# A float32 encoder trunk on one core: seven block products instead of eight for the first two up blocks of each MLP chunk

## The chip, the cores and the metric

The kernel runs on one core of one Trainium2 chip. The metric is the device time of one execution in microseconds. The engines are PE (TensorE: matmuls, with the loads of the stationary operand shown as PEld), DVE (VectorE), ACT (ScalarE), POOL (GpSimd) and SP (SyncE, which issues the loads of the weights). Each works through its own queue in program order and waits on semaphores.

## The reference

256 tokens of width 2048 pass two layers. Each layer has a mixer and then an MLP, both with an RMS norm in front and a residual add behind:

```
h = rmsnorm(x, norm_mix_w);  x = x + mixer(h)       # layer 0: retention and RG-LRU, layer 1: window attention
h = rmsnorm(x, norm_mlp_w)
u = relu(h @ w_up)           # 2048 -> 8192
x = x + (u * u) @ w_down     # 8192 -> 2048
```

The mixer ends with an output projection of 2048 columns, whose result is added to `x`. Everything is float32.

## The kernel before

**Tiling.** A block is 512 output columns over a contraction of 2048 (16 pieces `kt` of 128 rows), for both tiles of 128 tokens (`tt` 0 and 1). The program is a list of 89 blocks: 12 of the mixer's input, 4 residual blocks (`res`, numbered r0 to r3 here), 32 of an MLP, 5 of attention's input, 4 residual blocks, 32 of an MLP. An MLP runs in 4 chunks of 4 up blocks and 4 down blocks. The MLP's middle chunks are loops, the rest is written out.

**Precision.** Each float32 operand is split into a high part, which ACT rounds, and a rest, which DVE subtracts; a product is then three matmuls: high by high, high by low, low by high (lines 1399 to 1401). A block is read as 8 halves of two `kt`; a half is 12 matmuls of 128x128 by 128x512. For each half ACT makes `w_hi` (line 733, called a *hi* here) and DVE makes `w_lo` (line 976, a *lo*) from the raw weights in `raw`. Both have a ring of 4 halves, so ACT may make the *hi* of step k+4 when PE has done step k.

**Ticks.** ACT and DVE run a loop over the same steps: at tick k each first does what stands in `post` for the block before (evacuation, transposes, splitting), then the *hi* or *lo* of step k+4. What stands ahead of a *hi* or *lo* in its queue delays it.

**Pairs.** In the first three chunks of each MLP the four down blocks go as two pairs. Of the 2x2 blocks (two token tiles by the first four `kt` in two parts, by two column blocks) a pair makes seven products P1 to P7 of 6 matmuls each (`product`, lines 1425 to 1427) in place of two halves of two blocks (48 matmuls). The order of a pair's 20 steps is `PAIR_STEPS`: products, the halves 2 to 7 of the left (L) and the right (R) block, and an empty step. The products take token sums (`s_hi`, `s_lo`, made by `add_tokens`, `tokens`, `tokens_rest`) and weight sums, which DVE makes in `raw` (`add_weights`, lines 987 to 994). Four intermediate results are added to `x` by DVE (`add_part`, line 1003). R accumulates in `acc`, L in `bank`.

**Up blocks.** ACT takes an up block out of PSUM with the norm's scale and Relu (line 783), squares it in `stage` (line 788), DVE transposes it by 16 instructions of 32x256 into `turn` (line 1219), ACT and DVE split it into `b_hi` and `b_lo` (lines 741 and 1029), the stationary operands of the down blocks.

**Residual blocks.** DVE adds a residual block to `x` (line 1238), ACT takes its square sums (line 753), DVE transposes it by 16 instructions, ACT and DVE make `a_hi` (lines 743, 744) and `a_lo` (line 1033) with the norm's weights. The norm's factor is applied when an up block leaves. At the start of an MLP the first two up blocks are woven: PE does 6 halves of the first and 2 of the second before the two halves that need r3, and it waits for r0 to r2 before the first:

```
WOVEN_ORDER = ([(0, k) for k in range(6)] + [(1, 0), (1, 1), (0, 6), (0, 7)]
               + [(1, k) for k in range(2, 8)])
```

**Loads.** SP loads the weights by 1 MB (a unit: two halves) into four places of `raw`; each load waits until the *lo* of the last step that read its place is done.

Of the kernel before, what the change touches and what calls it, by code (L numbers as in the profile page):

```python
# [23 lines left out]
ACT = mybir.ActivationFunctionType  # L24
# [45 lines left out]
def mlp_blocks(last_kind):  # L70
    blocks = []
    for c in range(CHUNKS):
# [19 lines left out]
BY_QUADRANT = {"up", "res"} | DIRECT  # L92
# [9 lines left out]
QUADRANTS_PAIR = {6: 4, 7: 4, 8: 4, 9: 4}  # L102
# [7 lines left out]

PAIR_CHUNKS = CHUNKS - 1
PAIRS0 = {m + PERIOD * c + COLS + 2 * n for m in (MLP0, MLP1) for c in range(PAIR_CHUNKS) for n in range(2)}
PAIRS1 = {b + 1 for b in PAIRS0}
FIRST_PAIRS = {m + PERIOD * c + COLS for m in (MLP0, MLP1) for c in range(PAIR_CHUNKS)}
PAIR_STEPS = [("P", 1), ("L", 2), ("P", 5), ("L", 3), ("P", 2), ("P", 6), ("P", 4), ("L", 4), ("P", 7),
              ("L", 5), ("P", 3), ("R", 2), ("R", 3), ("R", 4), ("R", 5), ("R", 6), ("R", 7), (None, 0),
              ("L", 6), ("L", 7)]
PAIR_SPLIT = 17
STEP_OF = {what: k for k, what in enumerate(PAIR_STEPS)}
PAIR_UNITS = [("L", 0), ("R", 0), ("L", 1), ("L", 2), ("R", 1), ("R", 2), ("R", 3), ("L", 3)]  # L120
PAIR_FREE = [STEP_OF["P", 4] + 1, STEP_OF["P", 3] + 1, STEP_OF["L", 3] + 1, STEP_OF["L", 5] + 1,
             STEP_OF["R", 3] + 1, STEP_OF["R", 5] + 1, STEP_OF["R", 7] + 1, STEP_OF["L", 7] + 1]
# [3 lines left out]
LAST_TURNED_AT = STEP_OF["R", 6]  # L126
# [3 lines left out]
NSTEP = [PAIR_SPLIT if b in PAIRS0 else len(PAIR_STEPS) - PAIR_SPLIT if b in PAIRS1 else HALVES  # L130
         for b in range(NBLK)]
STEP0 = [sum(NSTEP[:b]) for b in range(NBLK + 1)]

# [14 lines left out]
def pair_step(b, k):  # L148

    if b in PAIRS0:  # L150
        return PAIR_STEPS[k]
    if b in PAIRS1:
        return PAIR_STEPS[PAIR_SPLIT + k]
    return None


def weight_at(b, k):

    what = pair_step(b, k)
    if what is None:  # L160
        return k // 2, k % 2, b + 1
    side, h = what
    first = b if b in PAIRS0 else b - 1
    if side == "P":
        q, e = PIECE_OF[h]
        return q, e, first + 1
    n = PAIR_UNITS.index((side, h // 2))
    return n % UNITS, h % 2, first + 1 + n // UNITS
WOVEN_ORDER = ([(0, k) for k in range(6)] + [(1, 0), (1, 1), (0, 6), (0, 7)]
# [70 lines left out]
SUMS_AT = {1: 0, 2: 1, 4: 2, 5: 3}  # L240
N_EVAC_ACT = total(BY_ACT, TT)
# [16 lines left out]
class Slot:  # L258
# [69 lines left out]
def build(nc, t):  # L328
    ctx = ExitStack()
    with ctx:  # L330
# [67 lines left out]
        place["at"] = 0  # L398
        kk_t = take(KV, SEQ)
# [12 lines left out]
        s_sum = take(4, 2, P)  # L412
# [89 lines left out]
        tokens_lo = sem("tokens_lo")  # L502

# [42 lines left out]
        def _(sp):  # L546
# [31 lines left out]
            def load(slot, view):  # L578

                b0 = slot.b  # L580
                for q in range(UNITS):
                    if b0 in PAIRS0:
                        side, g = PAIR_UNITS[q]
                        d = 0 if side == "L" else 1
                    elif b0 in PAIRS1:
                        side, g = PAIR_UNITS[UNITS + q]
# [5 lines left out]
                    if b0 in PAIRS1:  # L592
                        free = PAIR_FREE[q] - PAIR_SPLIT
                    elif b0 - 1 in PAIRS1:
                        free = PAIR_FREE[UNITS + q] - len(PAIR_STEPS)
                    else:
                        free = 2 * q + 2 - HALVES
# [116 lines left out]
        def _(act):  # L714
            def cut_hi(slot, n):
# [14 lines left out]
                if STEP0[slot.b] + n >= RING:  # L730
# [3 lines left out]
                                     ACT.Copy).then_inc(hi_ready, 2 if what == ("R", HALVES - 1) else 1)  # L734
# [25 lines left out]
            def leave(slot, kind, j):  # L760

                b = slot.b - 1
                act.wait_ge(half_used, slot.halves(late(b)))
# [5 lines left out]
                for tt in range(TT):  # L769
                    src = acc[:, b % 2, tt, :]  # L770
# [11 lines left out]
                    else:  # L782
                        ins = nc.scalar.activation(stage[:, tt, :], src, ACT.Relu if kind == "up" else ACT.Copy, scale=s)
                    ins.then_inc(evac_act, 1)
                if kind == "up":
# [63 lines left out]

            def post(slot, k):  # L850
                b = slot.b - 1
                if b < 0:
                    return
                kind, j = BLOCKS[b]
                if b - 1 + COLS in FIRST_PAIRS and k == 6:
                    tokens(slot)
                if k == late(b) and kind in BY_ACT:
                    leave(slot, kind, j)
                if k == 1 + late(b) and kind in ("res", "fin"):
                    act.wait_ge(evac_dve, slot.count(N_EVAC_DVE, 0))  # L860
                    square_sums(next_norm(b), j)
                if kind in SPLIT and k == out_at(kind, b):
                    hi, _, kt, scale = target(b)
                    for m in range(2):
                        turned_parts(hi, kt + 2 * m, None if scale is None else scale + 2 * m,
                                     slot.count(N_MOVED, -1, INIT_HALVES + m + 1), m, kind in BY_QUADRANT)
                if k == 4 and kind == "res" and j == COLS - 1:
# [89 lines left out]
        def _(dve):  # L957
# [8 lines left out]
            def cut_lo(slot, n):  # L966
# [5 lines left out]
                if what == (None, 0):  # L972
# [5 lines left out]
                                        ALU.subtract).then_inc(lo_ready, 2 if what == ("R", HALVES - 1) else 1)  # L978
# [18 lines left out]
            def add_part(slot, k):  # L997

                left, right = (slice((BLOCKS[slot.b + d][1]) * NB, (BLOCKS[slot.b + d][1] + 1) * NB) for d in (0, 1))
                for p, tt, cols, src in ((1, 0, left, 1), (5, 1, right, 0), (6, 0, right, 1), (7, 1, left, 1)):  # L1000
                    if k == STEP_OF["P", p]:
                        dve.wait_ge(half_used, slot.halves(k + 1))
                        nc.vector.tensor_tensor(x[:, tt, cols], x[:, tt, cols], accumulator(slot.b, src),
                                                ALU.add).then_inc(part_added, 1)

            def add_tokens(slot):

                a = turn[:, :, :].rearrange("p m (k t s) -> p m t k s", k=2, t=TT)
                (a11, a21), (a12, a22) = ([a[:, m, tt] for tt in range(TT)] for m in range(2))
# [6 lines left out]
                nc.vector.tensor_tensor(s4, a12, s2, ALU.subtract).then_inc(tokens_added, 1)  # L1016

# [176 lines left out]
            def turn_quadrants(slot, k, kind, j):  # L1194


                at = {tick + late(slot.b - 1): n for tick, n in quadrants_at(kind, slot.b - 1).items()}
# [11 lines left out]
                src = x[:, :, j * NB:(j + 1) * NB] if kind == "res" else stage  # L1209
# [13 lines left out]

            def plain_target(kind, j):
# [3 lines left out]
            def post(slot, k):  # L1228
                b = slot.b - 1
                if b < 0:  # L1230
                    return
                kind, j = BLOCKS[b]
                if k == late(b) and kind in ("res", "down", "fin"):
                    dve.wait_ge(half_used, slot.halves(late(b)))
                    for tt in range(TT):
                        c = BLOCKS[b + (b in PAIRS0) - (b in PAIRS1)][1]
                        xs = x[:, tt, c * NB:(c + 1) * NB]
                        nc.vector.tensor_tensor(xs, xs, accumulator(b, tt), ALU.add).then_inc(evac_dve, 1)
                if k == 1 + late(b):
# [18 lines left out]
                if kind in BY_QUADRANT:  # L1258
                    turn_quadrants(slot, k, kind, j)
# [475 lines left out]
```

## Time and profile before

| | before |
|---|---|
| time, median of 3 runs | 1993.46 us (1993.35 to 1993.85) |
| the profiled execution | 1995.09 us, its span 1993.3 us |
| PE busy | 1984.1 us (100%), 9089 instructions |
| PE weight loads | 1638.8 us (82%) |
| DVE busy | 1581.1 us (79%), 2190 instructions |
| ACT busy | 1066.0 us (53%), 1402 instructions |
| POOL busy | 45.1 us (2%) |
| HBM | 379.34 MB read, 191 GB/s over the span |

Busy times of different engines overlap. Matmuls are pipelined: a record lasts about 0.39 us, while the next one starts 0.227 us after it. In a timeline a row gives the start, the length (of several merged instructions, from the first's start to the last's end), the engine, the line, the operation and the tiles, and in brackets the idle time before it. The time between the starts of two instructions that follow each other without a wait is called their pace here; it is less than the duration.

### The profile page before, as it was taken

How to read it: one execution, taken by the hardware profiler on the slowest of the kernel's cores; microseconds unless marked ns; L12 is line 12 of the kernel's file. 1: busy time of each engine (PE TensorE's matmuls, PEld its weight loads, DVE VectorE, ACT ScalarE, POOL GpSimd, SP SyncE). 2: the span in 40 equal slices, each digit the busy share in tenths (PEclk: the TensorE clock that was granted, in tenths of full speed). 3: DMA queues.
4: the chain of work that ended last, by engine and by line, in shares of the span. 5: the costliest groups of instructions: out<-in, count | busy, mean ns of one | idle time of the engine just before them, and what ended most of it. 6: DMA issues, size and time to landing. Idle time of an engine off the chain costs nothing.

```text
span 1993.3 us, 25055 instructions
## 1 busy us (share of the span) xinstructions
PE 1984.1 (100%) x9089; PEld 1638.8 (82%) x9089; DVE 1581.1 (79%) x2190; ACT 1066.0 (53%) x1402; POOL 45.1 (2%) x55
## 2 busy tenths in 40 slices
PE   9999999999999999999999999999999999999998
PEld 7888888888888888888888878888888888888887
DVE  6777678989769868976889887989858876985875
ACT  6665665555445545544545566555445544544554
POOL 1110110000000000000000000000000000000000
PEclk9999999999999999999999999999999999999999
DMA  8556545655665475556655545564575555466563
GB/s 306 177 182 205 181 165 203 202 172 192 217 199 170 168 249 182 184 206 190 211 190 186 174 154 165 182 197 152 197 247 191 188 206 189 148 218 226 187 205 112
DMA packets 191758, 382.50 MB, mean 192 GB/s; under 512 B 6328, under 2 KB 7616, under 8 KB 191552
## 3 DMA queue, kind: packets, MB, share of 16 engines
q1 hardware_dynamic: 190288, 377.51, 56.5%
q0 software_dynamic: 1216, 3.88, 0.6%
q8 instruction: 48, 0.79, 0.2%
q14 instruction: 30, 0.25, 0.0%
q10 hardware_dynamic: 176, 0.07, 0.0%
HBM read 379.34 MB, written 2.10 MB: 191 GB/s over the span
## 4 chain that ended last, share of the span: by engine, by line
PE 98%; DVE 1%; issue 0%; ACT 0%; DMA 0%; ACTq 0%
PE acc L1399 26%; PE acc L1400 26%; PE acc L1401 26%; PE bank L1399 3%; PE bank L1400 3%; PE bank L1401 3%; PE acc L1426 1%; PE acc L1425 1%; PE acc L1427 1%; DVE area L1219 1%; PE bank L1427 1%; PE bank L1425 1%; PE bank L1426 1%; PE bank L1515 0%; PE bank L1592 0%; PE bank L1616 0%
## 5 line engine op out<-in xcount | busy, mean ns | idle before, releaser
L976 DVE TENSOR_TENSOR w_lo<-raw,w_hi 128x1024 fp32r<-128x1024 f32 x744 | 899.8, 1223 | 354.4 <-ACT w_hi L733 350.1
L733 ACT ACTIVATE w_hi<-raw 128x1024 fp32r<-128x1024 f32 x744 | 777.2, 1059 | 716.7 <-PE acc L1401 562.4
L1399 PE MATMUL acc<-w_hi,a_hi 128*128 128x512 f32 x1552 | 607.1, 391 | 0.0
L1401 PE MATMUL acc<-w_hi,a_lo 128*128 128x512 f32 x1552 | 604.1, 389 | 0.0
L1400 PE MATMUL acc<-w_lo,a_hi 128*128 128x512 f32 x1552 | 604.0, 389 | 0.0
L1399 PEld LDWEIGHTS acc<-w_hi,a_hi 128*128 128x128 f32 x1552 | 291.5, 188 | 61.2 <-issue 0.9
L1401 PEld LDWEIGHTS acc<-w_hi,a_lo 128*128 128x128 f32 x1552 | 291.4, 188 | 60.8
L1400 PEld LDWEIGHTS acc<-w_lo,a_hi 128*128 128x128 f32 x1552 | 291.4, 188 | 59.9
L1399 PE MATMUL acc<-w_hi,b_hi 128*128 128x512 f32 x784 | 305.7, 390 | 0.0
L1400 PE MATMUL acc<-w_lo,b_hi 128*128 128x512 f32 x784 | 305.3, 389 | 0.0
L1401 PE MATMUL acc<-w_hi,b_lo 128*128 128x512 f32 x784 | 305.0, 389 | 0.0
L1219 DVE STREAM_TRANSPOSE turn<-stage 32x256 f32<-32x256 f32 x512 | 223.0, 436 | 7.8
L1399 PEld LDWEIGHTS acc<-w_hi,b_hi 128*128 128x128 f32 x784 | 147.2, 188 | 32.2 <-issue 0.9
L1401 PEld LDWEIGHTS acc<-w_hi,b_lo 128*128 128x128 f32 x784 | 147.2, 188 | 30.7
L1400 PEld LDWEIGHTS acc<-w_lo,b_hi 128*128 128x128 f32 x784 | 147.2, 188 | 30.2
L1400 PE MATMUL bank<-w_lo,b_hi 128*128 128x512 f32 x288 | 112.5, 391 | 0.0
L1399 PE MATMUL bank<-w_hi,b_hi 128*128 128x512 f32 x288 | 112.5, 391 | 0.0
L1401 PE MATMUL bank<-w_hi,b_lo 128*128 128x512 f32 x288 | 112.3, 390 | 0.0
L741 ACT ACTIVATE b_hi<-turn 128x512 fp32r<-128x512 f32 x64 | 37.0, 625 | 112.5 <-DVE turn L1219 112.5
L1219 DVE STREAM_TRANSPOSE turn<-x 32x256 f32<-32x256 f32 x192 | 83.6, 435 | 2.9
L1399 PEld LDWEIGHTS bank<-w_hi,b_hi 128*128 128x128 f32 x288 | 54.0, 188 | 12.1
L1401 PEld LDWEIGHTS bank<-w_hi,b_lo 128*128 128x128 f32 x288 | 54.1, 188 | 11.7
(240 smaller groups left out, 1296.8 us busy)
## 6 DMA issues: line engine op xcount, KB each, us to landing
raw<-in_mlp_w_up SPq DMA_DIRECT2D x128, 1024.0 KB, 5.4
raw<-in_mlp_w_down SPq DMA_DIRECT2D x128, 1024.0 KB, 5.1
raw<-in_hyb_w_in SPq DMA_DIRECT2D x44, 1024.0 KB, 5.3
raw<-in_attn_w_qkv SPq DMA_DIRECT2D x20, 1024.0 KB, 5.1
raw<-in_hyb_w_out SPq DMA_DIRECT2D x16, 1024.0 KB, 5.2
raw<-in_attn_w_out SPq DMA_DIRECT2D x16, 1024.0 KB, 5.1
raw<-in_hyb_w_in SPq DMA_DIRECT2D x5, 512.0 KB, 9.6
out_y<-x SPq DMA_DIRECT2D x4, 512.0 KB, 3.0
```

The lines of the kernel that those rows point to most:

```text
L733: nc.scalar.activation(w_hi[:, ring(b, h)], raw[:, q, 2 * e:2 * e + 2, :], ACT.Copy).then_inc(hi_ready, 2 if what == ("R", HALVES - 1) else 1)
L741: nc.scalar.activation(hi[:, kt:kt + 2, :], src, ACT.Copy).then_inc(turned_hi, 1)
L976: nc.vector.tensor_tensor(w_lo[:, ring(b, h)], raw[:, q, 2 * e:2 * e + 2, :], w_hi[:, ring(b, h)].bitcast(F32), ALU.subtract).then_inc(lo_ ...
L1219: ins = nc.vector.transpose(dst[f * QUAD:(f + 1) * QUAD, :, :, a, :], src[a * QUAD:(a + 1) * QUAD, :, :, f, :])
L1399: nc.tensor.matmul(a, xh, wh, start=first, stop=False, skip_group_check=joins)
L1400: nc.tensor.matmul(a, xh, wl, start=False, stop=False, skip_group_check=joins)
L1401: ins = nc.tensor.matmul(a, xl, wh, start=False, stop=last, skip_group_check=joins)
L1425: nc.tensor.matmul(a, xh, wh, start=first, stop=False, skip_group_check=True)
L1426: nc.tensor.matmul(a, xh, wl, start=False, stop=False, skip_group_check=True)
L1427: ins = nc.tensor.matmul(a, xl, wh, start=False, stop=False, skip_group_check=True)
```

## The change

The first two up blocks of every chunk, in all four chunks of both MLPs, become a pair too (`UP0`, `UP1`), with an order of their own: the L block is finished first. The first pair of an MLP follows the residual blocks directly and takes r0 as the operand of its products; PE waits for r2 at L4 and for r3 at L6. The token sums of r0 are made once per MLP by DVE (`add_up_tokens`, from `a_hi + a_lo`), kept in `s_up`, and split into `s_hi` and `s_lo` again for each chunk, in the second down pair of the chunk before. The four intermediate results of an up pair are copied by DVE into `part_l` and `part_r`, the rest is added there (`sum_pair`), and ACT applies Relu in place.

The transposes change, too. For every up block but `UP0`, and for r1 to r3 of both layers, ACT writes 16 pieces of 32x256 to other partitions (`squares`, `move_res`: the square is made on the way, or a copy), in `shifted`; DVE then transposes by 4 instructions of 128x256 (`turn_shifted`). The ticks of these pieces stand in tables. The square sums and the norm of r3 go from ticks 1 to 5 to ticks 11 to 14.

The core of the diff:

```diff
-BY_QUADRANT = {"up", "res"} | DIRECT
+BY_QUADRANT = {"res"} | DIRECT
+BY_VECTOR = BY_QUADRANT | {"up"}
...
+QUADRANTS_UP = {3: 4, 4: 4, 6: 4, 7: 4}
+SQUARES_UP0 = {2: 2}
+SQUARES_UP1 = {1: 2, 2: 4, 3: 2, 4: 4, 5: 4}
+SQUARES_AT = {0: 4, 1: 6, 2: 6}
+SQUARES_PAIR = {3: 2, 4: 2, 5: 2, 6: 2, 7: 2, 8: 2, 9: 2, 10: 2}
+RES_AT = {2: 2, 3: 4, 4: 1, 5: 1, 6: 2, 7: 5, 8: 1}
+RES_MOVED_AT = {1: 4, 2: 4, 3: 4, 4: 4}
+LAST_SUMS_AT = 11
...
+UP0 = {m + PERIOD * c for m in (MLP0, MLP1) for c in range(CHUNKS)}
+UP1 = {b + 1 for b in UP0}
+DOWN0 = {m + PERIOD * c + COLS + 2 * n for m in (MLP0, MLP1) for c in range(PAIR_CHUNKS) for n in range(2)}
+DOWN1 = {b + 1 for b in DOWN0}
+PAIRS0, PAIRS1 = UP0 | DOWN0, UP1 | DOWN1
+MIXED = [("P", 1), ("L", 2), ("P", 5), ("L", 3), ("P", 2), ("P", 6), ("P", 4), ("L", 4), ("P", 7),
+         ("L", 5), ("P", 3), ("R", 2), ("R", 3)]
+DOWN_STEPS = MIXED + [("R", 4), ("R", 5), ("R", 6), ("R", 7), (None, 0), ("L", 6), ("L", 7)]
+UP_STEPS = MIXED + [("L", 6), ("L", 7), (None, 0), ("R", 4), ("R", 5), ("R", 6), ("R", 7)]
...
+UP_UNITS = [("L", 0), ("R", 0), ("L", 1), ("L", 2), ("R", 1), ("L", 3), ("R", 2), ("R", 3)]
...
+def squares_at(b):
+
+    if before_mlp(b):
+        return RES_AT
+    if moved_by_act(b):
+        return {k + late(b): n for k, n in RES_MOVED_AT.items()}
+    if b in UP0 | UP1:
+        return SQUARES_UP0 if b in UP0 else SQUARES_UP1
+    return SQUARES_PAIR if b + 1 in FIRST_PAIRS else {k + late(b): n for k, n in SQUARES_AT.items()}
+
...
+            def squares(slot, k):
+
+                b = slot.b - 1
+                at = squares_at(b)
+                if k not in at:
+                    return
+                if k == min(at):
+                    act.wait_ge(evac_act, slot.count(N_EVAC_ACT, 0))
+                if b in UP0:
                     for tt in range(TT):
-                        act.wait_ge(evac_act, slot.count(N_EVAC_ACT, -1, tt + 1))
-                        nc.scalar.activation(stage[:, tt, :], stage[:, tt, :], ACT.Square).then_inc(squared, 1)
+                        ins = nc.scalar.activation(part_l[:, tt, :], part_l[:, tt, :], ACT.Square)
+                    ins.then_inc(squared, 1)
+                    return
+                src = up_stage(b).rearrange("p t (k f c) -> p t k f c", k=COLS, f=QUADRANTS)
+                done = sum(n for tick, n in at.items() if tick < k)
+                for n in range(done, done + at[k]):
+                    a, f = divmod(n, QUADRANTS)
+                    ins = nc.scalar.activation(shifted[f * QUAD:(f + 1) * QUAD, a], src[a * QUAD:(a + 1) * QUAD, :, :, f, :],
+                                               ACT.Square)
+                if k == max(at):
+                    ins.then_inc(squared, 1)
+
+            def move_res(slot, k, j):
+
+                b = slot.b - 1
+                at = squares_at(b)
+                if k not in at:
+                    return
+                if k == min(at):
+                    act.wait_ge(evac_dve, slot.count(N_EVAC_DVE, 0))
+                src = x[:, :, j * NB:(j + 1) * NB].rearrange("p t (k f c) -> p t k f c", k=COLS, f=QUADRANTS)
+                done = sum(n for tick, n in at.items() if tick < k)
+                for n in range(done, done + at[k]):
+                    a, f = divmod(n, QUADRANTS)
+                    ins = nc.scalar.activation(shifted[f * QUAD:(f + 1) * QUAD, a], src[a * QUAD:(a + 1) * QUAD, :, :, f, :],
+                                               ACT.Copy)
+                if k == max(at):
+                    ins.then_inc(res_moved, 1)
...
+            def up_tokens(slot):
+
+                act.wait_ge(up_added, 1 if slot.b < MLP1 - 1 else 2)
+                if slot.b in DOWN0:
+                    act.wait_ge(half_used, slot.halves(STEP_OF["P", 3] + 1))
+                nc.scalar.activation(s_hi[:, :, :, :], s_up[:, :, :, :], ACT.Copy).then_inc(up_hi, 1)
...
+                b = slot.b
+                right = side_block(b, "R")
+                for p, side, tt, src in ((1, 0, 0, 1), (5, 1, 1, 0), (6, 1, 0, 1), (7, 0, 1, 1)):
                     if k == STEP_OF["P", p]:
                         dve.wait_ge(half_used, slot.halves(k + 1))
-                        nc.vector.tensor_tensor(x[:, tt, cols], x[:, tt, cols], accumulator(slot.b, src),
-                                                ALU.add).then_inc(part_added, 1)
+                        if b in UP0:
+                            ins = nc.vector.tensor_copy((part_l, part_r)[side][:, tt, :], accumulator(right, src))
+                        else:
+                            j = BLOCKS[b + side][1]
+                            xs = x[:, tt, j * NB:(j + 1) * NB]
+                            ins = nc.vector.tensor_tensor(xs, xs, accumulator(right, src), ALU.add)
+                        ins.then_inc(part_added, 1)
+
+            def sum_pair(slot, b):
+
+                part = up_stage(b)
+                dve.wait_ge(part_added, slot.pairs(4, 4, pair_of(b)[0]))
+                for tt in range(TT):
+                    nc.vector.tensor_tensor(part[:, tt, :], part[:, tt, :], accumulator(b, tt),
+                                            ALU.add).then_inc(pair_summed, 1)
+
...
+            def add_up_tokens(slot):
+
+                whole = part_l.rearrange("p t n -> p (t n)").rearrange("p (k s) -> p k s", k=4)
+                dve.wait_ge(turned_out, slot.count(N_TURNED, -1, INIT_HALVES))
+                link(nc.vector.tensor_tensor(whole, a_hi[:, 0:4, :].bitcast(F32), a_lo[:, 0:4, :].bitcast(F32), ALU.add))
+                (a11, a21), (a12, a22) = token_pieces(
+                    whole.rearrange("p (m k) (t s) -> p m t k s", m=2, t=TT))
+                s1, s2, s3, s4 = (s_up[:, n] for n in range(4))
+                link(nc.vector.tensor_tensor(s1, a21, a22, ALU.add))
+                nc.vector.tensor_tensor(s3, a11, a21, ALU.subtract)
+                link(nc.vector.tensor_tensor(s2, s1, a11, ALU.subtract))
+                nc.vector.tensor_tensor(s4, a12, s2, ALU.subtract).then_inc(up_added, 1)
+
+            def up_tokens_rest(slot):
+
+                dve.wait_ge(up_hi, slot.ups(1))
+                nc.vector.tensor_tensor(s_lo[:, :, :, :], s_up[:, :, :, :], s_hi[:, :, :, :].bitcast(F32),
+                                        ALU.subtract).then_inc(up_lo, 1)
 
...
+            def turn_shifted(slot, k, kind):
+
+                b = slot.b - 1
+                if b in UP0 or k != turn_at(kind, b):
+                    return
+                dve.wait_ge(turned_out, slot.count(N_TURNED, -1, INIT_HALVES))
+                if kind == "up":
+                    dve.wait_ge(squared, slot.count(N_SQUARED, 0))
+                else:
+                    dve.wait_ge(res_moved, sum(moved_by_act(n) for n in range(b + 1)))
+                dst = turn.rearrange("p m (k t a c) -> p t (m k) a c", k=2, t=TT, a=QUADRANTS)
+                for a in range(QUADRANTS):
+                    ins = nc.vector.transpose(dst[:, :, :, a, :], shifted[:, a])
+                ins.then_inc(turned, 2)
+
...
+                if slot.b - 2 in UP0 | UP1:
+                    behind(Slot(slot.b - 1, slot.i), NSTEP[slot.b - 1] + k)
+                behind(slot, k)
+
+            def behind(slot, k):
+
                 b = slot.b - 1
-                if b < 0:
-                    return
                 kind, j = BLOCKS[b]
-                if b - 1 + COLS in FIRST_PAIRS and k == 6:
-                    tokens(slot)
                 if k == late(b) and kind in BY_ACT:
                     leave(slot, kind, j)
...
+                if p == 5 and b in UP0:
+                    pe.wait_ge(up_lo, slot.ups(1))
...
-                    if b in FIRST_PAIRS and k == LAST_TURNED_AT:
+                    if (b in FIRST_PAIRS and what == ("R", 6)) or (b in (MLP0, MLP1) and what == ("L", 6)):
                         pe.wait_ge(turned_out, slot.count(N_TURNED, 0, INIT_HALVES))
+                    if b in (MLP0, MLP1) and what == ("L", 4):
+                        pe.wait_ge(turned_out, slot.count(N_TURNED, -1, INIT_HALVES))
```

## Rows read from the trace of the kernel before

**Rows 1.** The page, parts 1 and 2: busy time, and the granted clock by slices.
```profile
PE 1984.1 (100%) x9089; PEld 1638.8 (82%) x9089; DVE 1581.1 (79%) x2190; ACT 1066.0 (53%) x1402; POOL 45.1 (2%) x55
...
PEclk9999999999999999999999999999999999999999
```

**Rows 2.** The page, part 4: the chain that ended last, by engine.
```profile
PE 98%; DVE 1%; issue 0%; ACT 0%; DMA 0%; ACTq 0%
```

**Rows 3.** Waits: engine and line, releaser, us in total, times, longest.
```profile
ACT w_hi L733 <- PE acc L1401: 562.4, 369, 4.3
...
DVE w_lo L976 <- ACT w_hi L733: 350.1, 261, 4.1
...
PEld acc L1399 <- DVE w_lo L976: 0.3, 2, 0.2
```

**Rows 4.** Timeline of PE: first matmuls of blocks and of pairs.
```profile
342.31 0.39 PE L1399 MATMUL acc<-w_hi,b_hi 128*128 128x512 f32 x1
...
385.83 0.39 PE L1399 MATMUL acc<-w_hi,a_hi 128*128 128x512 f32 x1
...
472.87 0.39 PE L1425 MATMUL acc<-w_hi,b_hi 128*128 128x512 f32 x1
...
515.37 0.39 PE L1425 MATMUL acc<-w_hi,b_hi 128*128 128x512 f32 x1
...
1252.69 0.39 PE L1399 MATMUL acc<-w_hi,b_hi 128*128 128x512 f32 x1
```

**Rows 5.** Timeline of DVE around residual blocks, and token and weight sums.
```profile
345.92 1.28 DVE L1238 TENSOR_TENSOR x<-x,acc 128x512 f32<-128x512 f32 x2
...
348.25 1.78 DVE L1219 STREAM_TRANSPOSE turn<-x 32x256 f32<-32x256 f32 x4
...
359.11 1.67 DVE L1033 SCALAR_TENSOR_TENSOR a_lo<-turn,vecs,a_hi 128x256 fp32r<-128x256 f32 x4
...
360.69 3.50 DVE L976 TENSOR_TENSOR w_lo<-raw,w_hi 128x1024 fp32r<-128x1024 f32 x3
...
430.67 0.42 DVE L1011 TENSOR_TENSOR area<-turn 128x256 f32<-128x256 f32 x1
...
431.01 0.42 DVE L1012 TENSOR_TENSOR area<-turn 128x256 f32<-128x256 f32 x1
...
469.89 1.22 DVE L987 TENSOR_TENSOR raw<-raw 128x1024 f32<-128x1024 f32 x1
...
1260.49 1.28 DVE L1238 TENSOR_TENSOR x<-x,acc 128x512 f32<-128x512 f32 x2
```

**Rows 6.** Timeline of ACT: paces.
```profile
132.17 0.42 ACT L811 ACTIVATE b_hi<-area 128x256 fp32r<-128x256 f32 x1 [1.50 <-DVE area L1123]
...
132.49 1.04 ACT L733 ACTIVATE w_hi<-raw 128x1024 fp32r<-128x1024 f32 x1
...
345.29 1.06 ACT L733 ACTIVATE w_hi<-raw 128x1024 fp32r<-128x1024 f32 x1 [0.75 <-PE acc L1401]
...
347.23 0.64 ACT L753 ACTIVATE junk<-x 128x512 f32<-128x512 f32 x1 [0.88 <-DVE x L1238]
...
348.62 1.05 ACT L733 ACTIVATE w_hi<-raw 128x1024 fp32r<-128x1024 f32 x1
...
358.38 0.49 ACT L744 ACTIVATE a_hi<-turn,vecs 128x256 fp32r<-128x256 f32 x1
...
358.78 0.49 ACT L743 ACTIVATE a_hi<-turn,vecs 128x256 fp32r<-128x256 f32 x1
...
380.62 1.99 ACT L733 ACTIVATE w_hi<-raw 128x1024 fp32r<-128x1024 f32 x2
```

**Rows 7.** Timeline of the second down pair: DVE, PEld and PE at P4.
```profile
524.98 3.49 DVE L976 TENSOR_TENSOR w_lo<-raw,w_hi 128x1024 fp32r<-128x1024 f32 x3
...
526.25 0.19 PEld L1425 LDWEIGHTS bank<-w_hi,b_hi 128*128 128x128 f32 x1
...
526.39 0.40 PE L1425 MATMUL bank<-w_hi,b_hi 128*128 128x512 f32 x1
```

More of the change, by code:

```diff
@@ L125, with pair_of, unit_free, side_block @@
 SUM_COUNT = {5: 1, 7: 2, 6: 3, 4: 4}
-LAST_TURNED_AT = STEP_OF["R", 6]
+def pair_of(b):
+    first = b if b in PAIRS0 else b - 1
+    steps, units = (UP_STEPS, UP_UNITS) if first in UP0 else (DOWN_STEPS, DOWN_UNITS)
+    return first, steps, steps.index((None, 0)), units
+def unit_free(b, n):
+    _, steps, _, units = pair_of(b)
+    if n < 2:
+        return STEP_OF["P", 4 if n == 0 else 3] + 1
+    side, g = units[n]
+    return steps.index((side, 2 * g + 1)) + 1
+def side_block(b, side):
+    first = pair_of(b)[0]
+    return first + (side == ("R" if first in UP0 else "L"))
+LEFT = {side_block(b, "L"): (b in DOWN0 and b not in FIRST_PAIRS) for b in PAIRS0}
 WOVEN = ({MIX_OUT0, QKV0, ATT_OUT0}
          | {m + COLS * n for m in (MLP0, MLP1) for n in range(2 * CHUNKS)}) - PAIRS0
-NSTEP = [PAIR_SPLIT if b in PAIRS0 else len(PAIR_STEPS) - PAIR_SPLIT if b in PAIRS1 else HALVES
+NSTEP = [pair_of(b)[2] if b in PAIRS0 else len(pair_of(b)[1]) - pair_of(b)[2] if b in PAIRS1 else HALVES
          for b in range(NBLK)]
 STEP0 = [sum(NSTEP[:b]) for b in range(NBLK + 1)]
+def banks_of_blocks():
+    out, last = [], 1
+    for b in range(NBLK):
+        if b not in LEFT and not (b in DOWN0 and b not in FIRST_PAIRS):
+            last = 1 - last
+        out.append(last)
+    return out
+ACC_OF = banks_of_blocks()
 def ring(b, k):
@@ L148, in pair_step, with counts @@
 def pair_step(b, k):
[L150 to L154, printed above, removed]
+    if b not in PAIRS0 | PAIRS1:
+        return None
+    _, steps, split, _ = pair_of(b)
+    return steps[k + (split if b in PAIRS1 else 0)]
+def counts(b, k):
+    return 2 if b in PAIRS0 and k == NSTEP[b] - 1 else 1
 def weight_at(b, k):
@@ L240 @@
 SUMS_AT = {1: 0, 2: 1, 4: 2, 5: 3}
+N_PAIR_SUMS = [TT * sum(p < b for p in UP0 | UP1) for b in range(NBLK + 1)]
 N_EVAC_ACT = total(BY_ACT, TT)
@@ L398, in build @@
         place["at"] = 0
+        shifted = take(QUADRANTS, TT * NB // QUADRANTS).rearrange("p a (t k c) -> p a t k c", t=TT, k=COLS)
+        s_sum = take(4, 2, P)
+        s_up = take(4, 2, P)
+        part_l = take(TT, NB)
+        part_r = take(TT, NB)
+        place["at"] = 0
         kk_t = take(KV, SEQ)
@@ L762, in leave @@
                 b = slot.b - 1
-                act.wait_ge(half_used, slot.halves(late(b)))
+                if b not in UP0 | UP1:
+                    act.wait_ge(half_used, slot.halves(late(b)))
                 if b > 0 and BLOCKS[b - 1][0] in DIRECT:
@@ L1194, in turn_quadrants @@
             def turn_quadrants(slot, k, kind, j):
-                at = {tick + late(slot.b - 1): n for tick, n in quadrants_at(kind, slot.b - 1).items()}
+                at = quadrants_at(kind, slot.b - 1)
                 if k not in at:
@@ L1386, in products @@
                     side, h = what
-                    b = slot.b + (side == "L") - (slot.b in PAIRS1)
-                    begins = what == PAIR_STEPS[1]
+                    b = side_block(slot.b, side)
+                    begins = what == MIXED[1]
                 joins = what is not None
@@ L1401, in products @@
                         ins = nc.tensor.matmul(a, xl, wh, start=False, stop=last, skip_group_check=joins)
-                ins.then_inc(half_used, 2 if what == ("R", HALVES - 1) else 1)
+                ins.then_inc(half_used, counts(slot.b, k))
             def product(slot, k, p):
```

166 lines of the change are left out of this document (103 added, 63 removed).

## The prediction

> **What bounds the kernel now.** I read the busy table first: PE (TensorE's matmuls) is busy for 100% of the span, DVE for 79%, ACT for 53%, and the granted clock is full in every slice [rows 1]. The chain that ended last is 98% PE [rows 2]. The list of waits says who waits for whom: ACT's rounding to `w_hi` (a *hi*) waits 562 us for PE, DVE's subtraction to `w_lo` (a *lo*) 350 us for ACT, while PE's weight load waits 0.3 us for a *lo* in the whole run [rows 3]. So PE sets the time, the other two are paced by the four-deep ring behind it, and only two things move the end: fewer matmuls, or a *lo* that comes later than PE wants it. That needs the timeline at the places that change [rows 4 to 7].
>
> **What it removes.** Eight pairs of up blocks (two MLPs, four chunks) go from 16 halves of 12 matmuls (192) to 12 halves and seven products of 6 (186): 48 matmuls less. The trace prices it without a count. The four up blocks of a chunk take 472.87 - 385.83 = 87.04 us on PE, two of them 43.52; a down pair, the same work by seven products, takes 515.37 - 472.87 = 42.50 [rows 4]. One pair is worth 1.02 us, eight 8.2 us, if nothing waits. (Six matmuls less would be 6 x 0.227 = 1.36; the products fed from `s_hi` run a little slower, and the measured pairs hold that.) Per pair ACT gets 19 *hi* instead of 16, DVE 19 *lo* instead of 16, four weight sums, four part copies and four sums.
>
> **The six later pairs.** Their lead-in is the one that a second down pair has today: the pair before ends with L6, L7, the residual adds of its other side lie between the weight sums. The loads, as many and as large as now, wait on SP's queue at the same steps as a down pair's; in its second half L3's unit is fetched and used where a down pair has R2's, R2's and R3's follow and are used one step later than what they replace, or at the same. DVE runs through such a transition without a gap and is just in time: the *lo* of P4 ends at 524.98 + 1.22 = 526.20, the weight load that needs it starts at 526.25, and its matmul at 526.39 [rows 7], and all waits of PE for a *lo* come to 0.3 us [rows 3]. The part copies write what the residual adds of a down pair write and read less; I price them as those adds, 0.60 [rows 5]. So I cost these six at no stall, cover about 0.1 us; each tenth beyond it costs 0.6 us over the six. The second copy of the token sums (a *hi*- and a *lo*-sized operation) falls into the second down pair's last steps, where both engines idle for PE.
>
> **What hides the rest of each chunk.** Three of four up blocks have 4 transposes on DVE instead of 16 (16 x 0.447 = 7.2 us now, [rows 5]); PE never waited for them, so this buys nothing. ACT gets 16 squares of 32x256 per block instead of 2 of 128x512. Their price isn't in the trace. Below: the pace of 256-wide ACT work without a vector scale, 132.17 to 132.49 = 0.32 us; above: its whole duration, 0.42 [rows 6]. I take 0.32, the nearest row. The third up block's slot (21.76 us) then holds 8 *hi* 7.6, Relu 1.1, squares 5.1 (6.7 at 0.42), two *b_hi* pairs 2.1, tokens 1.0: 17 to 18.5 us on ACT, and the ring's lead of three halves (8.2 us) less 2.3 for a *hi* and a *lo* takes its bunching. DVE has some 18 us there. No cost; without that lead each us over would be a us of PE. The first down pair gets two squares per tick on ACT and loses 12 transposes on DVE; its *lo* come at most half a us later where they have 1.4 us or more in hand. No cost. Whole-width transposes (4 x 128x256): between 0.34 (pace of 256-wide DVE work, 430.67 to 431.01) and 0.447; I take 0.34 [rows 5].
>
> **The two starts.** Here the first pair of an MLP follows the residual blocks r0 to r3. Today the weave gives PE eight steps of 2.72 us there; the pair's steps are 1.36 to 2.72 us, want a *lo* each, and add four weight sums just before. Paces, start to start [rows 5, 6]: *lo* 1.14, *hi* 0.94, weight sum 1.13, residual add 0.60, `a_hi` 0.40, `a_lo` 0.40, square sums of a block 1.39 (347.23 to 348.62), move 0.32. Where an engine waits I add the gaps of the trace: 0.26 from a step's end to the *hi* (342.31 + 21.76/8 = 345.03 to 345.29 [rows 4, 6]), 0.19 from a *lo*'s end to the matmul [rows 7]. Walking the queues of before through r2, r3 and the first up block with these numbers gives its own starts within 0.3 us, and 0.1 us of stall in the second down pair, where there is none.
>
> First MLP, times from 385.83, the due start of P1. The slot of r2 starts at -43.52, DVE reaches the adds of r1 3.6 us later (345.92 - 342.31 [rows 4, 5]), as now. ACT then works through 16 moves, square sums and its *hi* with little idle time, and DVE gets 3 us of token sums: the adds of r2 end at -17.6. In r3's slot ACT does the token *hi* (to -16.9), then 16 moves 5.1, sums 1.4, three *hi* 2.9: *hi*(P1) starts at -7.5. Behind it one after the other: *lo*(P1) -6.4, weight sum -5.3, four transposes of r2 from -4.1, ACT's four `a_hi` from -2.75, *hi*(L2) -1.1, *lo*(L2) 0.0 to 1.2: just in time for L2 at 1.36. From there DVE has no gap: weight sum 1.1, *lo*(P5) 2.2, weight sum 3.4, *lo*(L3) 4.5 to 5.7, so L3 starts at 5.9, due 5.5: 0.4 late. Part copy 5.6, *lo*(P2) 6.2, weight sum 7.4, two adds of r3 8.5, *lo*(P6) 9.7 to 10.9: P6 starts at 11.1, due 10.0: 1.1 late. ACT may move r3 only after those adds: P4 0.45, L4 0.85 late. Then the queues catch up. Sum 2.85 us.
>
> Second MLP: the block behind attention ends later, so DVE comes to r1's adds 7.8 us into the slot of r2 (1260.49 - 1252.69 [rows 4, 5]) instead of 3.6. Moves leave no slack to win that back: *lo*(P1) is 1.85 us later, L2 waits 1.95, and the other stops add 2.9. Sum 4.9 us.
>
> The added wait at L4 (for r2) has all later steps of the pair behind it on PE, and ACT and DVE through the ring; r2 is turned about when P1 starts, L4 is due 14 us later: nothing. The wait at L6 for r3 is met with under 1 us in hand. The wait of P5 for the token *lo*, made in r3's slot: nothing. At 0.42 us per move the same walk gives 6.2 + 9.6 = 15.8 us; at 0.25 it gives 2.0 + 2.5.
>
> **Sum.** -8.2 + 2.85 + 4.9 = -0.5 us. The profiled execution took 1995.09 us (span 1993.3 and 1.8 around it), so 1994.6 for one like it; the runs' median, 1993.46, lies 1.6 lower, and there I forecast 1993.0, own range 1990 to 1996.5.
>
> **Rivals.**
> - *The starts cost nothing* (faster): ACT and DVE absorb them and the full 8.2 us stay: 1985.3; with only the P6 stop left at both, 1987.5. For it: DVE idles 350 us and ACT far more. Against: that idle time is spent waiting for PE, and DVE's back-to-back stretch from *lo*(P1) to *lo*(P6) is longer than the second down pair's by two adds, a turn and ACT's four `a_hi`, where that pair has 0.1 us to spare.
> - *The moves don't overlap* (slower): each one reads and writes another quarter of the partitions, and ACT starts the next when the last is done. For it: DVE's transposes by quadrant do this (pace 0.447, duration 0.44), while 256-wide DVE work in place has 0.34 [rows 5]. Against: no ACT row moves between quarters. Price 0.42 a move: -8.2 + 15.8 = +7.6, 2001.1. It decides against the change from about 0.33 us per move. The Trainium skill has a rule for VectorE (VectorE: DVE Perf Modes, Two Vector instructions with no wait between them): an instruction whose input or output starts in another quadrant than the one before is held until all earlier ones finish. The transposes agree with it (0.447 against 0.34). The page states it for VectorE; for ScalarE no run here shows it. ScalarE: Activation LUTs, What ACT_TABLE_LOAD costs, gives back-to-back overlap there without naming quadrants.
> - *The later pairs stall too*: 0.1 us of cover; one more 0.6 us DVE operation in each of six lead-ins gives +3.6, 1996.6. Against: I find none in the order of the queues.
>
> **Chances.** Forecast 0.43, starts free 0.20, moves don't overlap 0.29, later pairs 0.08. A change of 0.2% (4.0 us) is about what a measurement here can tell from none. The forecast gives nearly all to "within", a little to either side; the first rival to faster; the second nine in ten to slower; the third half to slower. Faster 0.24, within 0.40, slower 0.36. The range runs from 1985.0 to 2002.0: the second rival's price above, the first below.
>
> **What would show it.** 48 matmuls and no DMA less; 24 *hi* and *lo* more. Up pairs of later chunks at 42.5 us between first matmuls; the first pair of the first MLP at about 45.3, of the second at 47.4, with PE gaps before L3, P6, P4 and L4, and L2 in the second MLP. The pace of the moves tells the second rival (0.32 or 0.42). No gaps at both starts, or gaps of over 0.3 us in a later pair, would make the prediction wrong.

## The result and the profile after

The changed kernel takes 2005.16 us (median of 6 runs, 2004.95 to 2006.36) against 1993.65 us (1993.35 to 1995.98): ratio 1.0056, 95% interval 1.0043 to 1.0069. It is 11.5 us slower; 1993.0 was forecast, and the range ended at 2002.0. The profiled execution took 2004.95 us, its span 2003.2 us.

The page, the busy times, then the clock by slices:

```profile
PE 1980.8 (99%) x9041; PEld 1628.7 (81%) x9041; DVE 1528.6 (76%) x1968; ACT 1274.7 (64%) x1866; POOL 45.1 (2%) x55
...
PEclk9999999999999999999999999999999999999999
```

The 48 matmuls are gone and PE's busy time is 3.3 us less than in [rows 1], but the span is longer: PE now waits. The chain that ended last, by engine, says the same beside [rows 2]:

```profile
PE 91%; DVE 4%; ACT 3%; issue 1%; DMA 0%; ACTq 0%
```

PE's waits (line, releaser, us in total, times, longest). Before, a *lo* held up PE's weight loads for 0.3 us in all [rows 3] and none of its matmuls; here *lo* hold up its matmuls for 12.9:

```profile
PE bank L1633 <- DVE w_lo L1142: 11.3, 6, 4.6
...
PE acc L1633 <- DVE w_lo L1142: 0.9, 1, 0.9
PE bank L1661 <- DVE w_lo L1142: 0.7, 2, 0.4
```

Where they lie is read from the first matmuls of pairs and blocks, as in [rows 4]. Timeline of PE: first pair of the first MLP, the block behind it, first up pair of the second chunk, the block behind it, and the same start in the second MLP:

```profile
384.01 0.39 PE L1661 MATMUL acc<-w_hi,a_hi 128*128 128x512 f32 x1
...
434.62 0.39 PE L1633 MATMUL acc<-w_hi,a_hi 128*128 128x512 f32 x1
...
563.24 0.39 PE L1661 MATMUL acc<-w_hi,a_hi 128*128 128x512 f32 x1
...
605.74 0.39 PE L1633 MATMUL acc<-w_hi,a_hi 128*128 128x512 f32 x1
...
1299.86 0.39 PE L1661 MATMUL acc<-w_hi,a_hi 128*128 128x512 f32 x1
...
1352.32 0.39 PE L1633 MATMUL acc<-w_hi,a_hi 128*128 128x512 f32 x1
```

The up pair of the second chunk takes 42.50 us, as forecast, and so do the other five (42.49 to 42.51). The first pair of the first MLP takes 50.61 instead of 45.3, that of the second 52.46 instead of 47.4, and r3's slot ahead of the second one 1.18 more than 21.76. Against two blocks at 43.52: +7.1 + 8.9 + 1.2 - 6 x 1.02 = +11.1 us; the down pairs add 0.6, most of it in the first of each two. That is the 11.7 by which the stretch from the first MLP's start to the end of the last MLP's up blocks grew, and the medians' 11.5.

The largest gap of the first MLP, PE behind P1 (in the second MLP the same one is 4.8 us), and the one before L6:

```profile
385.14 0.39 PE L1663 MATMUL acc<-w_hi,a_lo 128*128 128x512 f32 x1
388.27 0.80 PE L1633 MATMUL bank<-w_hi,a_hi 128*128 128x512 f32 x1 [2.74 <-DVE w_lo L1142]
388.86 0.63 PE L1634 MATMUL bank<-w_lo,a_hi 128*128 128x512 f32 x1
389.29 0.63 PE L1635 MATMUL bank<-w_hi,a_lo 128*128 128x512 f32 x1
...
418.18 0.47 PE L1633 MATMUL bank<-w_hi,a_hi 128*128 128x512 f32 x1 [0.77 <-DVE w_lo L1142]
```

L2 was forecast just in time and is 2.9 us late; behind the gap the matmuls follow each other at 0.43 us instead of 0.227. The experiments below put the cause on ACT. Its timeline in r3's slot, moves of r2 (line 932) between square sums and *hi* (line 840):

```profile
368.01 1.70 ACT L932 ACTIVATE area<-x 32x256 f32<-32x256 f32 x4 [0.77 <-DVE x L1473]
369.72 0.63 ACT L860 ACTIVATE junk<-x 128x512 f32<-128x512 f32 x1
...
371.11 1.04 ACT L840 ACTIVATE w_hi<-raw 128x1024 fp32r<-128x1024 f32 x1
372.17 1.70 ACT L932 ACTIVATE area<-x 32x256 f32<-32x256 f32 x4
373.89 1.06 ACT L840 ACTIVATE w_hi<-raw 128x1024 fp32r<-128x1024 f32 x1
...
379.48 1.06 ACT L840 ACTIVATE w_hi<-raw 128x1024 fp32r<-128x1024 f32 x1
384.30 0.51 ACT L850 ACTIVATE a_hi<-turn,vecs 128x256 fp32r<-128x256 f32 x1 [3.76 <-DVE turn L1440]
```

Four moves last 1.70 us and one about 0.42 (0.416 on average over all 96), so the pace is (1.70 - 0.42)/3 = 0.427: a move starts when the one before it is done. The forecast took 0.32. The *hi* of P1 starts at 379.48, 4.5 us ahead of P1, where 7.5 were forecast. Then ACT stands idle for 3.76 us: `a_hi` of r2, which is ahead of the *hi* of L2 in its queue, waits for DVE's transposes. So the moves delay a start through the order of the queues too; no run tried another order.

### The profile page after: what moved, and what is told of

The parts are those of the page before. It is cut to its first block, busy times and chain, and to the rows that moved or that the text cites. A ratio compares the mean times of both kernels' runs of the same rounds, so it can differ in the third digit from the quotient of the medians.

```text
span 2003.2 us, 25376 instructions
## 1 busy us (share of the span) xinstructions
PE 1980.8 (99%) x9041; PEld 1628.7 (81%) x9041; DVE 1528.6 (76%) x1968; ACT 1274.7 (64%) x1866; POOL 45.1 (2%) x55
## 4 chain that ended last, share of the span: by engine, by line
PE 91%; DVE 4%; ACT 3%; issue 1%; DMA 0%; ACTq 0%
PE acc L1633 21%; PE acc L1634 21%; PE acc L1635 21%; PE bank L1633 5%; PE bank L1634 5%; PE bank L1635 5%; PE acc L1662 2%; PE acc L1661 2%; PE acc L1663 2%; DVE w_lo L1142 2%; ACT area L932 1%; ACT w_hi L840 1%; PE bank L1663 1%; PE bank L1661 1%; PE bank L1662 1%
## 5 line engine op out<-in xcount | busy, mean ns | idle before, releaser
L1633 PE MATMUL acc<-w_hi,a_hi 128*128 128x512 f32 x1232 | 483.0, 392 | 0.2
L1634 PE MATMUL acc<-w_lo,a_hi 128*128 128x512 f32 x1232 | 479.7, 389 | 0.0
L1635 PE MATMUL acc<-w_hi,a_lo 128*128 128x512 f32 x1232 | 479.6, 389 | 0.0
L1633 PEld LDWEIGHTS acc<-w_hi,a_hi 128*128 128x128 f32 x1232 | 231.3, 188 | 50.1 <-DVE area L1172 1.1
L1635 PEld LDWEIGHTS acc<-w_hi,a_lo 128*128 128x128 f32 x1232 | 231.3, 188 | 48.3
L1634 PEld LDWEIGHTS acc<-w_lo,a_hi 128*128 128x128 f32 x1232 | 231.3, 188 | 47.5
L915 ACT ACTIVATE area<-stage 32x256 f32<-32x256 f32 x256 | 106.3, 415 | 3.9
L1633 PE MATMUL bank<-w_hi,a_hi 128*128 128x512 f32 x192 | 77.0, 401 | 11.3 <-DVE w_lo L1142 11.3
L1634 PE MATMUL bank<-w_lo,a_hi 128*128 128x512 f32 x192 | 76.1, 396 | 0.0
L1635 PE MATMUL bank<-w_hi,a_lo 128*128 128x512 f32 x192 | 75.9, 395 | 0.0
```

The costliest lines, as they stand in the source:

```text
L915: ins = nc.scalar.activation(shifted[f * QUAD:(f + 1) * QUAD, a], src[a * QUAD:(a + 1) * QUAD, :, :, f, :], ACT.Square)
L1633: nc.tensor.matmul(a, xh, wh, start=first, stop=False, skip_group_check=joins)
L1634: nc.tensor.matmul(a, xh, wl, start=False, stop=False, skip_group_check=joins)
L1635: ins = nc.tensor.matmul(a, xl, wh, start=False, stop=last, skip_group_check=joins)
```

## The experiments

The edits are against the kernel after; the last one is against the fourth. The kernel before ran beside them: 1993.82 us (24 runs) beside the first four, 1993.58 (10 runs) beside the other three.

**Moves that stay in their quarter of the partitions.**

```diff
-ins = nc.scalar.activation(shifted[f * QUAD:(f + 1) * QUAD, a], src[a * QUAD:(a + 1) * QUAD, :, :, f, :], ...)
+ins = nc.scalar.activation(shifted[a * QUAD:(a + 1) * QUAD, f], src[a * QUAD:(a + 1) * QUAD, :, :, f, :], ...)
```

> All of ACT's moves and squares of 32x256 write to the same quarter of the partitions that they read (so the transposed blocks hold other elements). Theory A, a move that crosses quarters is held until the one before it is done: the pace of the moves falls from 0.43 us to about 0.33, the two starts are late by 3 and 5 us instead of 8.1 and 11.1, time about 1994.5 (1993 to 1996). Rival B, the shape sets the pace (32 partitions, runs of 32 elements): pace still 0.42, time 2005. Rival C, the moves are not what the starts wait for: pace 0.33, time still above 2002.

Measured: 1997.48 us (1996.69 to 1998.82), ratio to before 1.0017 (1.0008 to 1.0026). ACT, the moves of r1:

```profile
349.13 1.04 ACT L840 ACTIVATE w_hi<-raw 128x1024 fp32r<-128x1024 f32 x1
350.20 1.34 ACT L932 ACTIVATE area<-x 32x256 f32<-32x256 f32 x4
351.56 1.06 ACT L840 ACTIVATE w_hi<-raw 128x1024 fp32r<-128x1024 f32 x1
```

The shape is the same and the pace is (1.34 - 0.42)/3 = 0.31, so B is out. 7.7 us come back, so C is out. But A's 1994.5 was 3 us too low: the first pairs take 47.04 and 49.36 us, late by 4.5 and 6.9 against 42.5, where 3 and 5 were expected. The rows show one part of the rest: between a *hi* and a group of moves nothing overlaps (349.13 to 350.20 is 1.07 us, where *hi* follows *hi* after 0.94; the group hands over after 1.36, where four paces are 1.23). That is 0.25 us for each such group, three times per block. The first of a block's four groups reads and writes the first quarter, where instructions of 128 partitions start too, and it does overlap with its neighbours:

```profile
367.30 1.04 ACT L1002 ACTIVATE s_hi<-area 128x1024 fp32r<-128x1024 f32 x1
368.25 1.32 ACT L932 ACTIVATE area<-x 32x256 f32<-32x256 f32 x4
369.48 0.62 ACT L860 ACTIVATE junk<-x 128x512 f32<-128x512 f32 x1
```

It starts 0.95 us after the instruction before it and hands over after 1.23. So what costs the 0.25 us is again another starting quarter, not the change from one kind of work to another.

**Without the moves of the residual blocks.**

```diff
-if moved_by_act(b):
-    move_res(slot, k, j)
...
-    dve.wait_ge(res_moved, sum(moved_by_act(n) for n in range(b + 1)))
+    dve.wait_ge(evac_dve, slot.count(N_EVAC_DVE, 0))
...
-    ins = nc.vector.transpose(dst[:, :, :, a, :], shifted[:, a])
+    ins = nc.vector.transpose(dst[:, :, :, a, :], shifted[:, a] if kind == "up" else xs[:, :, :, a, :])
```

> ACT moves no residual block; DVE's four whole-width transposes read x itself (so a and its blocks hold other elements). The pairs, their steps and waits stay. Theory A: without the 6.8 us of moves in each of the three slots only DVE's own stretch before P6 is late, 1.5 us at each start, time about 1989 (1987.5 to 1991). Rival C, the lead-in of the pair itself (weight sums, part copies, adds of r3) makes the starts late: 1998 or more.

Measured: 1988.77 us (1988.53 to 1990.69), ratio 0.9974 (0.9963 to 0.9985). Both first pairs take 43.96 us, 1.5 late each; PE's waits for a *lo*, in the form used above:

```profile
PE acc L1661 <- DVE w_lo L1140: 1.6, 2, 0.8
```

That is P6, as the walk of the queues had it: the stop there costs 1.1 us. The rest of the 1.5 comes before P4 (0.3), not before L3 (0.05), where the walk had 0.4. The moves of the residual blocks make nearly all of the loss. And even with moves that cost nothing a first pair is no gain: 43.96 against 43.52 for two woven blocks [rows 4].

**The gap behind P1 filled with matmuls.**

```diff
+if p == 1 and b in (MLP0, MLP1):
+    for _ in range(10 if b == MLP0 else 18):
+        nc.tensor.matmul(bank[:, 3, :], a_hi[:, 0, 0:P], a_hi[:, 0:2, :]..., start=True, stop=True)
```

> The kernel after, and behind P1 of the first pair of each MLP 10 (first MLP) or 18 (second) extra matmuls into a free bank, in the time in which PE waits for L2. Theory D, the lower granted clock behind the gap costs 1.5 us at each start: L2 runs at 0.227 us per matmul, time about 2002. Theory A, ACT and DVE set the starts: the clock stays up, but the time comes back as gaps before L3 (0.4) and P6 (1.1), the first pair still takes 50.6 us between first matmuls, time 2005 within 0.6.

Measured: 2006.64 us (2005.46 to 2007.02), profiled 2005.46 against 2004.95. The median lies 1.5 us above that of the kernel after, outside the 0.6 that A allowed. In the profiles the stretch from the first MLP's start to the end of the last MLP's up blocks is 1525.1 us in both, so this isn't seen at the starts; it stays open. The granted clock in two stretches of the kernel after (stretch and length, busy time and instructions of PE, PEld, DVE, ACT and POOL, then the clock as a share of full speed, DMA share, GB/s):

```profile
386.00:388.00 2.00, 0.00 (x0) 0.00 (x0) 1.94 (x4) 2.00 (x4) 0.00 (x0) 0.94 0.00 0
388.00:390.00 2.00, 1.73 (x4) 1.45 (x5) 2.00 (x3) 1.80 (x2) 0.00 (x0) 0.50 0.00 0
```

and in the kernel with the filled gap, with two of the gaps that it has instead:

```profile
388.00:390.00 2.00, 1.53 (x7) 1.04 (x6) 2.00 (x3) 2.00 (x3) 0.00 (x0) 1.00 0.00 0
```

```profile
388.78 0.50 PE L1633 MATMUL bank<-w_hi,a_hi 128*128 128x512 f32 x1 [0.47 <-DVE w_lo L1142]
...
398.52 0.50 PE L1661 MATMUL acc<-w_hi,s_hi 128*128 128x512 f32 x1 [0.82 <-DVE w_lo L1142]
```

Behind 2.9 us without a matmul the clock was at its lower level of 1.2 GHz for the next six; with PE kept busy it stayed at 2.4 GHz. A gap alone doesn't say which: in the run with moves in their quarter PE stops for 2.8 us before L2 in the second MLP, and the clock stays at 2.4 GHz:

```profile
1300.21 0.50 PE L1633 MATMUL bank<-w_hi,a_hi 128*128 128x512 f32 x1 [2.63 <-DVE w_lo L1142]
```

```profile
1300.00:1302.00 2.00, 1.79 (x8) 1.49 (x9) 2.00 (x3) 1.74 (x2) 0.00 (x0) 1.00 0.00 0
```

With the gap filled the first pairs still take 50.59 and 52.47 us, as after: D is out, A holds. L2 starts 4.26 us into the first MLP's pair in both; here PE is through it earlier and then waits for the *lo* of L3 and P6, where the kernel after had no gap. So here the lower clock cost nothing, since the other engines were later than PE.

**Up pairs in chunks 1 to 3 only.** The edit, cut to its core; the loops over middle chunks begin one chunk later, and the token sums of r0 are made in the first chunk's third up slot.

```diff
-UP0 = {m + PERIOD * c for m in (MLP0, MLP1) for c in range(CHUNKS)}
+UP0 = {m + PERIOD * c for m in (MLP0, MLP1) for c in range(1, CHUNKS)}
...
 def moved_by_act(b):
-    return any(m - COLS < b < m for m in (MLP0, MLP1))
+    return False
...
-if slot.b + 2 in (MLP0, MLP1) and k == 3:
+if slot.b - 2 in (MLP0, MLP1) and k == 6:
     add_up_tokens(slot)
```

> Up pairs in chunks 1 to 3 only; the first chunk of each MLP is woven as before, residual blocks are transposed by DVE as before, up blocks are still squared and moved by ACT. Theory A, the loss is all at the two starts: six pairs of 42.5 us instead of 43.52, no gap of PE over 0.3 us in them, time 6 us below the kernel before, about 1988. Rival E, the moves and the second copy of the token sums cost something in every chunk: 1991 to 1994.

Measured: 1989.88 us (11 runs, 1987.76 to 1990.69), ratio to before 0.9977 (0.9968 to 0.9986): faster than both kernels, 3.9 us below before, where 6 were expected. In the profile the stretch from the first MLP's start to the end of the last MLP's up blocks is 5.2 us shorter. Its second chunk:

```profile
555.77 0.39 PE L1665 MATMUL acc<-w_hi,a_hi 128*128 128x512 f32 x1
...
598.31 0.39 PE L1637 MATMUL acc<-w_hi,a_hi 128*128 128x512 f32 x1
```

All six pairs take 42.49 to 42.54; the down pairs lose 0.0 to 0.3 each, 0.8 in all. In the profile theory A holds, with a small part of E; the median lies between the two, 1.9 us above A's 1988 and 1.1 below E's 1991. That the medians show 1.3 us less than the profile is within the scatter of the runs (2.9 us).

**The rule behind the pace.** Three residual blocks moved in another order, the rest as after:

```diff
 a, f = divmod(n, QUADRANTS)
-ins = nc.scalar.activation(shifted[f * QUAD:(f + 1) * QUAD, a], src[a * QUAD:(a + 1) * QUAD, :, :, f, :], ...)
+to, at_to = {MLP0 - 3: (a, f), MLP0 - 2: ((a + 1) % QUADRANTS, f), MLP1 - 3: (f, a)}.get(b, (f, a))
+if b == MLP0 - 3:
+    a, f = f, a
+    at_to = a
+if b == MLP1 - 3:
+    a, f = f, a
+ins = nc.scalar.activation(shifted[to * QUAD:(to + 1) * QUAD, at_to], src[a * QUAD:(a + 1) * QUAD, :, :, f, :], ...)
```

`MLP0 - 3` is r1 and `MLP0 - 2` r2 of the first MLP, `MLP1 - 3` r1 of the second; `a` is the quarter read, `to` the quarter written.

> The kernel after, with the moves of three residual blocks in another order (other elements): r1 of the first MLP: four moves one after the other write to one quarter, the quarter read changes from move to move; r2 of the first MLP: the quarter read and the quarter written differ, but both stay the same for four moves; r1 of the second MLP: each move reads and writes one and the same quarter, another one than the move before. All other moves as after. Theory A1, a move is held when its input or its output starts in another quarter than that of the move before: pace 0.43, 0.31, 0.43. Rival A2, a move is held because it crosses quarters: 0.43, 0.43, 0.31. Rival A3, only a change of the quarter written holds it: 0.31, 0.31, 0.43.

Measured: 2002.97 us (one run). ACT, the first four moves of each of the three blocks:

```profile
345.30 1.70 ACT L938 ACTIVATE area<-x 32x256 f32<-32x256 f32 x4 [0.88 <-DVE x L1479]
...
367.89 1.34 ACT L938 ACTIVATE area<-x 32x256 f32<-32x256 f32 x4 [0.77 <-DVE x L1479]
...
1262.67 1.70 ACT L938 ACTIVATE area<-x 32x256 f32<-32x256 f32 x4 [1.75 <-DVE x L1479]
```

Paces 0.427, 0.307, 0.427: A1 alone fits. The fourth case, in which only the quarter written changes, is the kernel after, with 0.427. Crossing quarters costs nothing if it stays the same crossing; what holds a move is that its input or its output starts in another quarter than that of the move before. Each of a block's 16 pieces has its own pair of quarters, so one of the two changes at every step in whatever order. The Trainium skill states this for VectorE (VectorE: DVE Perf Modes, Two Vector instructions with no wait between them); ACT's rows agree, 0.427 against 0.307.

**DVE's transposes put back, all eight up pairs kept.**

```diff
 def squares_at(b):
-    if before_mlp(b):
-        return RES_AT
...
 def moved_by_act(b):
-    return any(m - COLS < b < m for m in (MLP0, MLP1))
+    return False
```

> The kernel after, but r1 to r3 are transposed by DVE in 16 instructions each, as before, and ACT moves none of them; all eight up pairs stay. Theory A, a start has room for these blocks on neither engine: 7.2 us per block more on DVE, which had no gap there, PE late by about 8 and 11 us at the two starts (above all before P4 and P7), time 2005 (2002 to 2008), as after. Rival F, the moves on ACT are all the harm: no more than 3 us in all, time below 1991.

Measured: 2011.85 us (2009.34 to 2012.24), ratio 1.0083 (1.0066 to 1.0099). F is out; A's direction holds and its size doesn't: the slots of r2 and r3 and the first pair are late by 13.1 us at the first MLP and by 13.2 at the second, where 8 and 11 were expected. PE at P7 in the first MLP:

```profile
406.22 0.39 PE L1633 MATMUL bank<-w_hi,a_lo 128*128 128x512 f32 x1
409.77 0.77 PE L1659 MATMUL acc<-w_hi,s_hi 128*128 128x512 f32 x1 [3.17 <-DVE area L1170]
410.34 0.63 PE L1660 MATMUL acc<-w_lo,s_hi 128*128 128x512 f32 x1
```

It waits for a part copy that stands behind the 16 transposes and the `a_lo` of r3 on DVE. The lower clock follows for 14 matmuls (0.2 us each), and no gap of the pair comes behind it that would have taken them anyway. So of the two ways to serve a first pair, in the orders that were run, the moves are the cheaper (2005.2 against 2011.9).

**The moves alone.** Up pairs in chunks 1 to 3, woven first chunks, but r1 to r3 moved by ACT:

```diff
 def moved_by_act(b):
-    return False
+    return any(m - COLS < b < m for m in (MLP0, MLP1))
```

> The kernel with up pairs in chunks 1 to 3 only and woven first chunks, but r1 to r3 moved by ACT (16 moves each) as after. Theory A, the moves hurt only where the pair's short steps follow them: no gap at the first MLP, at the second at most the 1.2 us that r3's slot showed after; time 1990.5 (1989.5 to 1992). Rival F: the moves alone make PE wait 5 us or more at each start, time above 1996.

Measured: 2001.61 us (1999.0 to 2003.0), ratio 1.0036 (1.0025 to 1.0048), 11.7 us above the same kernel with DVE's transposes. A fell and F's time holds: the moves hurt under the woven start as well, by another wait. DVE's adds and `a_lo` of r2, then PE's last matmul of r3 and first of the MLP:

```profile
366.60 1.28 DVE L1477 TENSOR_TENSOR x<-x,acc 128x512 f32<-128x512 f32 x2
...
384.02 1.68 DVE L1241 SCALAR_TENSOR_TENSOR a_lo<-turn,vecs,a_hi 128x256 fp32r<-128x256 f32 x4 [0.98 <-ACT a_hi L855]
```

```profile
383.71 0.39 PE L1639 MATMUL acc<-w_hi,b_lo 128*128 128x512 f32 x1
385.80 0.47 PE L1637 MATMUL acc<-w_hi,a_hi 128*128 128x512 f32 x1 [1.71 <-issue]
```

PE waits not for a *lo* but for the block itself: the row names no releaser (`issue`), and `a_lo` ends at 385.70, 0.10 us before PE goes on. From the start of the adds to the end of `a_lo` it takes 19.1 us, where the kernel before takes 15.3:

```profile
366.50 1.28 DVE L1238 TENSOR_TENSOR x<-x,acc 128x512 f32<-128x512 f32 x2
...
380.14 1.67 DVE L1033 SCALAR_TENSOR_TENSOR a_lo<-turn,vecs,a_hi 128x256 fp32r<-128x256 f32 x4
```

The moves of one block and the *hi* between them are one chain on ACT, which has no gap from the first move to the last; orders with fewer *hi* in between were not run. PE stops 1.9 and 2.1 us in the first MLP, 3.7 and 1.0 in the second, with 13 matmuls at the lower clock (2.6 us) behind the third stop and 1.0 us in r3's slot.

## Why the prediction was wrong

- *One pair is worth 1.02 us* and *six later pairs without a stall*: right (42.50 us, no gap).
- *What hides the rest of each chunk: no cost*: right within 0.14 us per first down pair. With moves that stay in their quarter those take 42.51 instead of 42.53 to 42.63, so that rest too is the pace of the squares.
- *Their price: I take 0.32, the nearest row*: this step failed. That row is a pair of 128-partition instructions, which start in the same place; the rows that resemble a move were DVE's transposes by quarter, at pace and duration alike. The second rival was the case, and what was held against it, that no ACT row moves between quarters, was no evidence for either. That rival's wording needs one change: a move is held not because it crosses quarters but because each move starts in another one than the move before. Going from 0.31 to 0.427 costs 7.7 us (2005.2 against 1997.5, squares included).
- *Late by 2.85 + 4.9 us at 0.32, 6.2 + 9.6 at 0.42*: measured 4.5 + 6.9 at 0.31 and 8.1 + 11.1 (with r3's slot) at 0.427. So the walk was 3.5 us short in all at either pace, which, with the 0.6 of the down pairs, is why the time lies 4 us above the 2001.1 that it gave the second rival. (Its terms for the first start add to 2.8, not 2.85.) About half of it was put at nothing: *the wait at L6 is met with under 1 us in hand*. PE stops there at both starts and at either pace, 0.8 to 0.9 us each, because the *lo* of L6 stands behind r3's transposes and `a_lo` on DVE (the row at 418.18 above). Each restart of PE costs 0.1 us more (the first matmul behind a gap is followed after 0.33 us, not 0.227, in each of some five stops), and the walk's paces between *hi* and moves were too short (above). With no moves to do its sum was right (1.5 us), in part by luck: L3 lost less than it had, P4 more. The rest, under 1 us, wasn't taken apart.
- *PE gaps before L3, P6, P4 and L4, and L2 in the second MLP*: after, they stand before L2, P4, L4 and L6 in both MLPs; L3 and P6 appear as soon as PE is through L2 earlier (moves in their quarter, filled gap).
- *The added wait at L4: nothing*: right by itself, as at L6; PE's waits there name *lo*. Whether the later waits saved anything isn't shown: under the woven start, which wants r2 at once, the same moves cost 11.7 us.
- *The second MLP is later, by r1's adds*: right in direction; its r3 slot lost 1.2 us, which the sum put at zero.

## What to carry to other kernels

Small instructions that shuffle data between quarters of the partitions have to be priced at their whole duration on ACT as on DVE, and so has the change to other work that starts in another quarter. Saving PE work pays where the other engines have been waiting for PE, so the same edit is worth 1 us in a running chunk and loses 7 to 9 at a start that waits for data from the stage before: make it where the operands have long been there. A late block must be followed on two paths, its share of an engine's time and its own chain from input to operand.

## What the runs showed of the hardware

On ACT a 32x256 instruction follows the one before it after 0.307 us if both its input and its output start in the same quarters as that one's, also when these two differ, and after 0.427 us, its whole duration, if either changes. The same holds between a 32x256 move and a *hi* of 128 partitions: 0.25 us more for a group of four in any quarter but the first. Behind a gap of PE of 2.9 us six matmuls ran at 1.2 GHz, behind one of 3.7 us 13, behind one of 4.8 us seven, and behind one of 2.8 us none; so the length of a gap alone didn't tell what it cost, and where another engine was later than PE it cost nothing.
